# A third place for cast weight slabs at the openings of four dense stages, filled in the normalisation ahead, and the Silu table loaded at the opening

## The reference

```python
h = x
for layer in range(2):
    if layer % 2 == 0:
        mix = dsa_mixer(h, ...)      # x @ w_in first (5 column tiles of 128)
    else:
        mix = hgrn2_mixer(h, ...)    # x @ w_in first (32 column tiles)
    h = layer_norm(ALPHA * h + mix, ln_g[layer, 0], ln_b[layer, 0])
    ffn = (silu(h @ w_gate) * (h @ w_up)) @ w_down    # 1024 -> 2816 -> 1024
    h = layer_norm(ALPHA * h + ffn, ln_g[layer, 1], ln_b[layer, 1])
```

## Time and profile before

| | |
|---|---|
| median of 3 runs | 1926.43 us |
| profiled execution | 1926.61 us, span 1924.5 us, mean granted TensorE clock 0.973 |
| PE busy | 1822.6 us (95%), 12584 matmuls |
| PE weight load busy | 1428.9 us (74%) |
| DVE busy | 900.1 us (47%) |
| ACT busy | 836.6 us (43%) |
| POOL busy | 244.5 us (13%) |
| DMA | 133.97 MB, mean 70 GB/s |

### The profile page before, as it was taken

The page is one execution under the profiler, slowest core; times in us unless marked ns, Lnnn a source line. Parts: engine busy times, 40 slices in busy tenths (PEclk is TensorE's granted clock), DMA queues, the critical chain, the costliest instruction groups (busy, mean ns, idle before and its releaser), DMA issues. The chain is left out here.

```text
span 1924.5 us, 31502 instructions
## 1 busy us (share of the span) xinstructions
PE 1822.6 (95%) x12584; PEld 1428.9 (74%) x12584; DVE 900.1 (47%) x1642; ACT 836.6 (43%) x1380; POOL 244.5 (13%) x205
## 2 busy tenths in 40 slices
PE   6999999899989899999999999999997999999997
PEld 5686666576766666778888888788886878888885
DVE  2663554555576796343333332554554533333233
ACT  4543444455442445344344322765552354444222
POOL 3011222000125000120000000322220210000000
PEclk9998999899998899999999999999997999999998
DMA  5221101200121000213323333222220223333331
GB/s 183 88 93 62 35 24 35 83 23 12 47 81 33 1 1 1 77 55 98 98 87 100 97 99 98 64 85 77 67 67 23 88 69 95 98 98 98 97 94 50
DMA packets 38486, 133.97 MB, mean 70 GB/s; under 512 B 4896, under 2 KB 5344, under 8 KB 38112
## 3 DMA queue, kind: packets, MB, share of 16 engines
q1 hardware_dynamic: 37504, 130.07, 21.7%
q10 hardware_dynamic: 864, 2.23, 0.3%
HBM read 129.40 MB, written 2.10 MB: 68 GB/s over the span
## 5 line engine op out<-in xcount | busy, mean ns | idle before, releaser
L140 DVE TENSOR_TENSOR big_parts<-ring,big_parts 128x1024 fp32r<-128x1024 f32 x172 | 214.8, 1251 | 530.5 <-ACT big_parts L135 529.1
L166 PE MATMUL bank<-h_parts,big_parts 128*128 128x512 f32 (+1 forms) x1000 | 395.4, 395 | 11.6 <-DVE big_parts L140 6.5
L167 PE MATMUL bank<-y_parts,big_parts 128*128 128x512 f32 (+1 forms) x1000 | 389.4, 389 | 0.0
L168 PE MATMUL bank<-h_parts,big_parts 128*128 128x512 f32 (+1 forms) x1000 | 389.1, 389 | 0.0
L135 ACT ACTIVATE big_parts<-ring 128x1024 fp32r<-128x1024 f32 x172 | 182.1, 1060 | 293.6 <-PE bank L168 290.5
L166 PEld LDWEIGHTS bank<-h_parts,big_parts 128*128 128x128 f32 x1000 | 188.3, 188 | 59.8 <-issue 14.6
L168 PEld LDWEIGHTS bank<-h_parts,big_parts 128*128 128x128 f32 x1000 | 188.6, 189 | 39.4
L167 PEld LDWEIGHTS bank<-y_parts,big_parts 128*128 128x128 f32 x1000 | 188.7, 189 | 36.7
L166 PE MATMUL bank<-big_parts 128*128 128x512 f32 x352 | 136.9, 389 | 0.0
L167 PE MATMUL bank<-work_parts,big_parts 128*128 128x512 f32 x352 | 136.9, 389 | 0.0
L168 PE MATMUL bank<-big_parts 128*128 128x512 f32 x352 | 136.9, 389 | 0.0
(11 more groups left out here) (400 smaller groups left out, 2844.5 us busy)
## 6 DMA issues: line engine op xcount, KB each, us to landing
ring<-in_wstream SPq DMA_DIRECT2D x229, 512.0 KB, 3.6
x<-in_xt SPq DMA_DIRECT2D x8, 512.0 KB, 6.9
out_t<-x SPq DMA_DIRECT2D x8, 256.0 KB, 2.0
work<-in_memt ACTq DMA_DIRECT2D x1, 1024.0 KB, 14.0
y<-in_cw SPq DMA_DIRECT2D x1, 1024.0 KB, 4.9
cst<-in_cst ACTq DMA_DIRECT2D x1, 768.0 KB, 7.9
cos<-in_reset SPq DMA_DIRECT2D x2, 256.0 KB, 6.7
big<-work SPq DMA_DIRECT2D x4, 128.0 KB, 4.7
```

The source lines that it names most:

```text
L140: dve.tensor_tensor(self.parts[:, self.place_of(n), 1, :, :], self.ring[:, n % RING, :, :], self.parts[:, self.place_of(n), 0, :, :].bitca ...
L166: pe.matmul(out, w[0], x[0], start=start, stop=False, skip_group_check=True)
L167: pe.matmul(out, w[0], x[1], start=False, stop=False, skip_group_check=True)
L168: return pe.matmul(out, w[1], x[0], start=False, stop=stop, skip_group_check=True)
```

## The change

`Ctx` gets a third place (`place_third`) for one given slab; its cast waits for no slab. It is set for slab 2 of `stage_dsa_in` (tiles 24 to 27 of `big`) and of both FFN stages (tiles 20 to 23); `stage_hgrn` has three places already. The normalisations ahead of the four stages cast and split three slabs in place of two, and slab 2's cast and split are taken out of the openings. In `stage_ffn` the first turn of ACT's and DVE's loops is written out, without slab 2, and the loops run from 1; and ACT loads the Silu table at the start of the stage, ahead of `Apply`.

```diff
--- before.py
+++ after.py
@@ -122,6 +122,16 @@
         flat = self.workr if place is None else place.rearrange("p a b -> p (a b)")
         self.parts = flat[:, tile * T:(tile + 4 * held) * T].rearrange("p (s a k c) -> p s a k c", s=held, a=2, k=KT)
         self.first, self.held = 0, held
+        self.third = {}
+
+    def place_third(self, n, tile):
+
+        at = self.bigr[:, tile:tile + 4, :].rearrange("p a b -> p (a b)")
+        self.third = {n: at.rearrange("p (a k c) -> p a k c", a=2, k=KT)}
+
+    def place(self, n):
+
+        return self.third[n] if n in self.third else self.parts[:, self.place_of(n), :, :, :]
 
     def place_of(self, n):
 
@@ -130,15 +140,15 @@
     def cast_slab(self, act, n, i=0):
 
         act.wait_ge(self.slab_ready[n % RING], 16 * (n // RING + 1) + i * 16)
-        if n >= self.held:
+        if n >= self.held and n not in self.third:
             act.wait_ge(self.slab_done, n - self.held + 1 + i * RING)
-        act.activation(self.parts[:, self.place_of(n), 0, :, :], self.ring[:, n % RING, :, :], ACT.Copy).then_inc(self.slab_cast, 1)
+        act.activation(self.place(n)[:, 0, :, :], self.ring[:, n % RING, :, :], ACT.Copy).then_inc(self.slab_cast, 1)
 
     def split_slab(self, dve, n, i=0):
 
         dve.wait_ge(self.slab_cast, n + 1 + i * RING)
-        dve.tensor_tensor(self.parts[:, self.place_of(n), 1, :, :], self.ring[:, n % RING, :, :],
-                          self.parts[:, self.place_of(n), 0, :, :].bitcast(F32), ALU.subtract).then_inc(self.slab_split, 1)
+        dve.tensor_tensor(self.place(n)[:, 1, :, :], self.ring[:, n % RING, :, :],
+                          self.place(n)[:, 0, :, :].bitcast(F32), ALU.subtract).then_inc(self.slab_split, 1)
 
     def slab_wait(self, pe, n, i=0):
 
@@ -146,7 +156,7 @@
 
     def slab_parts(self, n, k):
 
-        return self.parts[:, self.place_of(n), 0, k, :], self.parts[:, self.place_of(n), 1, k, :]
+        return self.place(n)[:, 0, k, :], self.place(n)[:, 1, k, :]
 
     def raw_slab(self, n, k):
 
@@ -1774,7 +1784,7 @@
         act.wait_ge(self.root, 1)
         act.activation(st[:, 3, :], st[:, 2, :], ACT.Sqrt, bias=c.eps[:, self.eps:self.eps + 1]).then_inc(self.root, 1)
         if ahead:
-            for n in range(PARTS):
+            for n in range(3):
                 c.cast_slab(act, ahead + n)
 
     def vector(self, dve, ahead=None):
@@ -1858,6 +1868,9 @@
     return 22, None
 
 
+FFN_THIRD, DSA_THIRD = 20, 24
+
+
 def ffn_parts(c):
 
     return 24, c.bigr[:, :, :]
@@ -1876,6 +1889,7 @@
     def after():
 
         c.place_parts(*next_parts(c))
+        c.place_third(slab + KT + 2, FFN_THIRD)
         return slab + KT
 
     with nc.Block() as block:
@@ -1937,6 +1951,7 @@
     def next_stage():
 
         c.place_parts(*dsa_parts(c))
+        c.place_third(slab + slabs + 2, DSA_THIRD)
         return slab + slabs
 
     with c.nc.Block() as block:
@@ -2027,11 +2042,13 @@
                     mm = product(pe, c.bank[u][:, :], c.slab_parts(gu + u, k), xp.tile(k), k == 0, k == KT - 1)
                 mm.then_inc(c.slab_done, 1)
 
+            c.place_third(gu + 2, FFN_THIRD)
             warm(c, pe, c.bank[4], 10)
             first_pair(c, pe, gu, xp)
             xp.wait_banks(pe)
             for u in range(2, 4):
                 gate_up(u, 0)
+            c.third = {}
             with pe.Fori(1, FT // 2) as i:
                 for u in range(4):
 
@@ -2055,16 +2072,23 @@
 
         @block.scalar
         def _(act):
-            xp.scalar(act)
-            with act.Fori(0, FT // 2) as i:
+            def turn(i, first):
+
                 for u in range(2):
                     c.slab_done_wait(act, gu + 2 * u, i)
-                    c.cast_slab(act, gu + 2 * u + PARTS, i)
+                    if u or not first:
+                        c.cast_slab(act, gu + 2 * u + PARTS, i)
 
                     act.activation(silu[:, u, :], c.bank[2 * u][:, :], ACT.Silu).then_inc(silu_out, 1)
                     c.cast_slab(act, gu + 2 * u + 1 + PARTS, i)
                     act.wait_ge(prod_out, i * 2 + (u + 1))
                     act.activation(hid[:, i * 2 + u, :], prod[:, u, :], ACT.Copy).then_inc(cast_out, 1)
+
+            act.preload_act_table(ACT.Silu)
+            xp.scalar(act)
+            turn(0, True)
+            with act.Fori(1, FT // 2) as i:
+                turn(i, False)
             act.preload_act_table(ACT.Sqrt)
             for s in range(FT):
                 if s + PARTS < FT:
@@ -2081,11 +2105,12 @@
 
         @block.vector
         def _(dve):
-            xp.vector(dve)
-            with dve.Fori(0, FT // 2) as i:
+            def turn(i, first):
+
                 for u in range(2):
                     for v in range(2):
-                        c.split_slab(dve, gu + 2 * u + v + PARTS, i)
+                        if u or v or not first:
+                            c.split_slab(dve, gu + 2 * u + v + PARTS, i)
                     dve.wait_ge(silu_out, i * 2 + (u + 1))
                     c.slab_done_wait(dve, gu + 2 * u + 1, i)
                     dve.tensor_tensor(prod[:, u, :], silu[:, u, :], c.bank[2 * u + 1][:, :], ALU.mult).then_inc(prod_out, 1)
@@ -2093,6 +2118,11 @@
                     dve.wait_ge(cast_out, i * 2 + (u + 1))
                     dve.tensor_tensor(hid_lo[:, i * 2 + u, :], prod[:, u, :], hid[:, i * 2 + u, :].bitcast(F32), ALU.subtract)\
                        .then_inc(hidden_out, 1)
+
+            xp.vector(dve)
+            turn(0, True)
+            with dve.Fori(1, FT // 2) as i:
+                turn(i, False)
             made = 0
             for s in range(FT):
                 if s + PARTS < FT:
@@ -2172,6 +2202,7 @@
     tables = ((c.cos[:, :], c.sin[:, :], "inv_q"), (cosi, sini, "inv_i"))
     kdst = wk(c, 20 * T, T)
     c.place_parts(*dsa_parts(c))
+    c.place_third(n0 + 2, DSA_THIRD)
     xp = Apply(c, "dx")
     cqp = TileParts(c, "di_cq", v["cq"], c.bigr[:, 28:30, :], c.bigr[:, 30:32, :])
 
@@ -2261,7 +2292,8 @@
 
             for t in range(2):
                 c.slab_done_wait(act, n0 + t)
-                c.cast_slab(act, n0 + t + PARTS)
+                if t:
+                    c.cast_slab(act, n0 + t + PARTS)
                 act.activation(v["cq"][:, t, :], c.bank[t][:, :], ACT.Copy).then_inc(root_out, 1)
                 act.activation(sq[:, t, :], c.bank[t][:, :], ACT.Square).then_inc(sq_out, 1)
             c.cast_slab(act, n0 + 4)
@@ -2338,7 +2370,8 @@
                 dve.tensor_scalar(si, ang[:, 0, :], 3.1415925, -3.1415925, ALU.min, ALU.max).then_inc(tab, 1)
                 dve.wait_ge(tab, 2 * i + 1)
                 dve.scalar_tensor_tensor(co, si, -1.0, si, ALU.mult, ALU.max).then_inc(tab, 1)
-                c.split_slab(dve, n0 + PARTS + i)
+                if i:
+                    c.split_slab(dve, n0 + PARTS + i)
             c.split_slab(dve, n0 + 4)
 
             dve.wait_ge(root_out, 3)
@@ -2722,7 +2755,6 @@
                     c.cast_slab(act, n0 + u + HG_HELD)
 
             xp.scalar(act)
-            c.cast_slab(act, n0 + 2)
             act.wait_ge(lb_s, 2)
             act.activation(lb[:, 1:3, :], lb[:, 1:3, :], ACT.Exp).then_inc(lb_s, 1)
             for s in range(HG + 1):
@@ -2876,7 +2908,6 @@
                 dve.scalar_tensor_tensor(y[:, h, :], o_bank[:, :], vec(c, "g_norm"), sg[h % 2], ALU.mult, ALU.mult).then_inc(y_out, 1)
 
             xp.vector(dve)
-            split(2)
             decays()
             dve.wait_ge(c.reset_in, 16)
             dve.wait_ge(clear, 1)
```

## The result

| | median, us | runs | profiled execution | its span | mean granted clock |
|---|---|---|---|---|---|
| before, beside it | 1926.35 | 7 (1923.97 to 1928.59) | 1926.61 | 1924.5 | 0.973 |
| after | **1911.63** | 7 (1911.17 to 1920.38) | 1911.24 | 1909.5 | 0.979 |

The ratio is 0.9935, with an interval of 0.9923 to 0.9948. The kernel is 14.7 us faster; 12.2 were forecast, and 1911.63 lies at the low end of the range.

The account below looks back on a forecast made before the run. PE's order of work was taken as the bound, with gaps waiting mostly on slab 2. Terms -6.78 - 3.44 - 2.07 - 1.77 + 1.89 = -12.17 took 1926.6 to 1914.4, stated as 1914.5 us; range 1911 to 1919.5.

Parts of the forecast that it names:

- Part 1: Both FFN stages: slab 2 cast and split ahead removes PE's gap, -3.39 us each; slab 3 stays hidden.
- Part 2: Both FFN stages: half-clock drops behind the 3.23 us gaps go with them, -1.72 us each; none follows the shorter gap.
- rival A: The clock loss stays or returns elsewhere: 1916.2 us with one drop left, 1917.9 with both; chance 0.18.
- Part 3: stage_dsa_in: PE's gap before slab 2 goes, -2.07 us; slab 3 is ready with only 0.4 us to spare.
- Part 4: stage_hgrn: ACT reaches the Sigmoid that frees PE's bank earlier without slab 2's cast and split, -1.77 of 2.31 us.
- Part 5: Third splits ending four normalisations: +0.71 us before stage_dsa_in, nothing before first FFN and stage_hgrn, +1.18 before second FFN; +1.89.
- rival B: Every third split is on the path in all four normalisations: +4.72 instead of +1.89 us, 1917.3; chance 0.09.
- Parts 6 to 8: FFN Silu preload, written-out first loop turn and slab 6's later DMA load: preload and loop taken as zero, load beside independent work.
- part 7: FFN loops entered at turn 1 after a written-out turn: taken as 0, with 1.8 us slack; losing table loads gains nothing.
- rival D: ACT or DVE stalls entering the FFN loop at its second turn; slower than before only from 7.9 us per entry; chance 0.03.
- part 8: Slab 6's DMA load waits for slab 2's split, starting in the opening beside ACT and DVE work not needing it.
- rival C: PE finds slab 2 ready but waits for something else there, only costs sure: 1925 to 1928 us; chance 0.06.

Follow-up runs that it names:

- experiment 4: Kernel after without the hand-placed Silu table load at the opening of both FFN stages; 1912.32 us over 9 runs, ratio 0.9941.
- experiment 5: Kernel after with stage_hgrn's slab 2 cast and split put back in its opening; 1913.04 us over 6 runs, ratio 0.9937.
- experiment 7: Kernel after with slab 2's split moved from the four normalisations to the openings, its cast left there; 1911.06 us (ratio 0.993), run again 1904.76 us (0.9897).

## Why the prediction came out as it did

**Part 1 (FFN gaps, -3.39 each): right.** The gaps are gone, slab 3 was in time, and with the other parts the stretches fit within 0.02: 379.08 - 3.39 - 1.72 = 373.97, measured 373.96; 377.62 - 3.39 - 1.72 + 1.18 = 373.69, measured 373.67.

**Part 2 (the drops behind them, -1.72 each): right in size and cause,** shown by the filler, 1.64 and 1.65. What failed is its reason: "none follows the shorter one". Over all traces in which a gap of 1.9 to 2.2 us was left open behind the first pair, a drop followed in 5 of 9. The profile on which the prediction rested had 0 of 2.

It is tempting to make a missing term of this: 2 x 5/9 x 1.7 = 1.9 us, and the three pairs of medians on one chip give gains of 14.7, 13.7 and 13.9, on average 1.9 more than the 12.2 forecast. The stretches don't bear it out. `stage_dsa_in` took 306.0 to 306.1 in the three traces with a drop behind its open gap and 307.3 in the one without; `stage_hgrn` took 319.9 and 318.4 with one, 320.0, 318.7 and 318.5 without. The clock lost over the whole stretch was no larger with it either (12.0 us against 15.4, and 10.2 against 10.2 to 12.0). That the two numbers are alike is chance. What the traces do give: the four touched stretches add up to 1384.0 in both executions of before and to 1371.0 to 1371.3 in four of the kernel after, 12.9 less for a forecast of 12.2. The 0.7 more comes from one execution of before in which a drop held up the opening of the second FFN (5.83), so that the third split cost nothing by comparison. The other 1.2 us of the medians aren't in the touched stretches of any trace. The code that the change doesn't touch took 536.8 to 542.5 us in the traces, in no order by kernel; how much of the 1.2 is chance in it stays open.

The rule of the Trainium skill that rival A named (TensorE: Matmul & The Clock Gate, Part 1: the activity monitor runs free of the kernel) agrees with the trace in so far as the same gap has a drop behind it in one execution and none in another. What rival A made of it, that the FFN drops could be missing in some executions and the median gain less, did not come: they were there in 4 of 4 places.

**Part 3 (`stage_dsa_in`, -2.07 + 0.71): right only where a drop lies on the spreading.** Root to slab 2 went from 22.26 to 20.87 in experiments 4 and 5, which is -1.39 for -1.36, and in all three executions the spreading ran at half clock. The kernel after itself did not get there: 22.36 to 22.57 in all four of its traces, where code as before has 21.80 to 21.82 with the spreading at full clock. The third split costs 1.14 then in place of 0.71, and the drop on the fillers 1.5 to 1.7. So the second half of rival A, a loss that comes back at another place, came true here: the gap and the half clock that could follow it are gone, and half clock ahead of the first pair has come. The stretch is still shorter, by 0.3 to 0.7 (305.4 to 305.7 for 306.0 to 306.1). The margin of 0.4 for slab 3 was real, too: an opening 1.14 earlier turned it into a wait of 0.67.

**Part 4 (`stage_hgrn`, -1.77): right by the arithmetic, by an accident of the trace.** From opening to slab 2 it is 19.72 before and 18.07 after, -1.65; the rest of the chain was read rightly, with 0.49 left where some 0.3 was named. Compared with an opening at full clock the part is worth 0.53, since the cost beside it was wrong, as follows.

**Part 5 (third splits, +1.89): the sum nearly right for these executions, the reasoning of "nothing" wrong.** Between the two profiled executions the openings moved by +0.65, 0, -0.29 and +1.14, 1.5 in all. The prediction took PE's lateness of 1.4 us ahead of the first FFN and of `stage_hgrn` for a property of the code ("the same code behind the same kind of matmul stream"). It is the clock. The openings in the table above fall into a plain pattern: with PE at full clock a stage opens 4.4 to 4.5 us behind the root with two splits, 5.55 to 5.63 with three and mostly 6.70 with a fourth pass, so DVE is always last; with a drop on the spreading and two splits it opens at 4.9 in `stage_dsa_in` (8 matmuls) and 5.83 to 5.93 elsewhere (16), and elsewhere the third split hides behind it. The row that the prediction had, 0.18 us for a matmul of 128x128 (2.88 for 16), was itself the slow pace; in experiment 5 and in the kernel after the same 16 take 1.95, 0.12 each, ahead of `stage_hgrn`. The trace of before had the fast pace as well, ahead of the second FFN, where the prediction looked at DVE alone:

```profile
1530.65 1.95 PE L1767 MATMUL bank<-cst,work 128*128 128x128 f32 x16
```

Ahead of the first FFN every trace with up to three splits opens at 5.84 to 5.87, so the drop lay there each time, and the zero held. Ahead of `stage_hgrn` it lay there in both executions of before, in neither of the two with fillers and in none behind the change: the price of +1.13 is real, and is masked in the profile by the drop that went. With it the sum for all four is some +3.0 and the forecast 1915.6, further off. So the forecast came nearer by luck, and rival B, every third split on the path, is right wherever the spreading runs at full clock: in all but the first FFN.

**Parts 6 to 8: right.** The preload costs nothing and gains nothing (experiment 4): Identity starts at 832.01, on DVE's release. The Trainium skill (ScalarE: Activation LUTs, What ACT_TABLE_LOAD costs) has a drain of some 1.4 us behind the load, by which Identity could start at 832.7 at the earliest; the measurement decides. The loops did lose their table loads, as part 7 left open. Groups of ACT by line, first the kernel before and then after (count, busy us, mean ns; idle ahead):

```profile
L135 ACT ACT_TABLE_LOAD x22 | 28.2, 1283 | 42.8 <-PE bank L168 42.8
L2064 ACT ACT_TABLE_LOAD x22 | 28.2, 1283 | 0.4
```

```profile
L2087 ACT ACT_TABLE_LOAD x2 | 2.6, 1283 | 5.0 <-PEq L92 5.0
```

44 loads of 1.28 us became 2, 54 us less for ACT, and the time did not move for it. They go with the written-out first turn, not with the preload: experiment 4 has 2 as well. ACT waits for PE there. The loop's entry brought no stall (rival D), and slab 6's later load (part 8) no wait: the FFN stretches leave 0.02 us for both. PE found slab 2 ready, so rival C is out, too.

**What was not forecast at all.** -4.03 in front of the first root and +1.7 behind the last are no effect of the change. Over all traces the same code up to the first root took 518.4 to 523.4 us with no order by kernel (before 522.81 and 519.92; after 518.78, 518.40, 519.76 and 519.74), and the last stretch 17.7 to 17.8 or 19.4. Whoever had put the 15.4 us between the two profiled executions down to the change would have counted 2.3 us of chance. In `stage_dsa_in` part of the gain is lost again in some executions: experiment 5 reaches slab 2 1.40 earlier than before did, and its whole stretch is 307.29 against 307.32. One more drop stands in it; whether the earlier start brings such drops or they are chance can't be told from these traces.

## What to carry to other kernels

A gap on PE costs its length and can bring half clock behind it: 1.64 us for each gap of 3.2 us here, nothing that the whole stretch shows for those of 2. Price both, and take the clock of gaps from several executions, not from one. Ask, too, where the change makes PE wait anew: here the later opening of `stage_dsa_in` came with 1.5 to 1.7 us of half clock on the fillers, in all four profiled executions. Before a cost is hidden under "PE is later anyway", look at the granted clock of that stretch: a cover that is a clock drop is not there every time. Work that moves ahead of a barrier should go there only on engines that have time before it: here the split was the last to end and the cast was not, and dividing the two gave the lowest median of all versions (1905.9), with four of 11 times above 1916 all the same.

## What the hardware showed beyond that

- **Drops differ in place and number from execution to execution of one kernel, and the time follows them.** The kernel after took 1911.2, 1914.7 and 1920.4 us at mean granted clocks of 0.979, 0.976 and 0.973. In the profiled executions 36.9 to 51.9 us of clock were lost in all ((1 - granted clock) x time), for the kernel before once 51.9 and once 45.2.
- **A later release can cost more than its delay.** Four passes of 1.22 us on DVE in front of four stages cost 9 to 10 us.
- **Filler matmuls in a gap took the drop away.** With 7 or 13 of 128x256 f32 in a gap of 3.2 us behind the first pair none followed, in 4 of 4 places. They took 0.42 us each at full clock, and the 7 fitted into the wait.
- **A split and POOL's low part at one time slow each other.** In experiment 7 the low part beside the split took 2.04 us in the FFNs, where those before it took 1.30; in `stage_dsa_in` it took 2.29, and the split itself 2.33 in place of 1.22.
